# Forming the low half of every fourth transposed block on TensorE and copying it out with ScalarE

## The reference, cut to what matters

```
sc = jnp.einsum('bqkgd,bqjkd->bqkgj', qg, kg).astype(jnp.float32) * scale
sc = jnp.where(valid[:, :, None, None, :], sc, -jnp.inf)
p = jax.nn.softmax(sc, axis=-1).astype(v.dtype)
o = jnp.einsum('bqkgj,bqjkd->bqkgd', p, vg)
```

## Time and profile before

| | us |
|---|---|
| Median of 3 runs | 3589.48 (3582.31, 3589.48, 3591.34) |
| The profiled execution's own time | 3584.13 |
| Its span in the trace | 3582.3 |
| PE busy in the span | 3170.6 (89%) |
| Weight loads busy | 2670.9 (75%) |
| DVE busy | 2083.1 (58%) |
| ACT busy | 1833.1 (51%) |
| POOL busy | 781.8 (22%) |

### The profile page before, as it was taken

One profiled execution on the slowest core, in us unless ns is written; L12 is line 12 of the kernel. 1 busy time (PEld: TensorE's weight loads), 2 busy tenths in 40 slices (PEclk: granted clock), 3 DMA queues, 4 the chain that ended last, 5 costly groups with the idle time before them and its releaser, 6 DMA issues. The chain is left out here.

```text
span 3582.3 us, 51698 instructions
## 1 busy us (share of the span) xinstructions
PE 3170.6 (89%) x17464; PEld 2670.9 (75%) x17464; DVE 2083.1 (58%) x5173; ACT 1833.1 (51%) x3664; POOL 781.8 (22%) x1091
## 2 busy tenths in 40 slices
PE   2999949999949899999399997899969999969998
PEld 1788848888837777778267775899858888859997
DVE  2577648888825556564499986544336666642112
ACT  2566536767735565666377775211136666643221
POOL 1544421111123221211011101111014444311110
PEclk8999979999979999999699998899979999979999
DMA  6466672243172222222621112544342222144332
GB/s 138 144 207 202 194 184 55 57 105 74 38 241 80 77 74 63 78 66 76 120 49 39 29 31 73 168 142 141 124 162 67 70 70 71 41 127 150 118 118 71
DMA packets 345285, 370.25 MB, mean 103 GB/s; under 512 B 68384, under 2 KB 289360, under 8 KB 340288
## 3 DMA queue, kind: packets, MB, share of 16 engines
q1 hardware_dynamic: 331184, 318.39, 32.0%
q0 software_dynamic: 13840, 48.58, 4.2%
HBM read 216.10 MB, written 150.80 MB: 102 GB/s over the span
## 5 line engine op out<-in xcount | busy, mean ns | idle before, releaser
L76 PE MATMUL i_p_g<-i_hT_lo,i_wh 128*128 128x512 f32 x768 | 310.7, 405 | 5.5 <-issue 5.0
L78 PE MATMUL i_p_g<-i_hT_hi,i_wh 128*128 128x512 f32 x768 | 306.9, 400 | 0.0
L77 PE MATMUL i_p_g<-i_hT_hi,i_wl 128*128 128x512 f32 x768 | 306.2, 399 | 0.0
L1509 DVE SCALAR_TENSOR_TENSOR i_score<-i_relu,i_w,i_score 128x1024 f32<-128x1024 f32 (+7 forms) x154 | 156.1, 1024 | 194.5 <-ACT i_relu L1383 192.2
L1394 ACT ACTIVATE i_above<-i_score,i_less 128x384 bf16<-128x384 f32 (+13 forms) x140 | 182.9, 1306 | 91.6 <-POOL i_less L1460 70.9
L1028 DVE TENSOR_TENSOR mla_tl<-mla_p_t,mla_th 128x512 fp32r<-128x512 f32 (+1 forms) x320 | 186.1, 606 | 45.1 <-ACT mla_th L1071 43.2
L998 DVE CUSTOM_DVE_ANT_0 dsa_probs<-dsa_p_s,dsa_mask 128x512 f32<-128x512 f32 (+3 forms) x320 | 184.6, 605 | 42.2 <-PE dsa_p_s L1638 40.6
L1071 ACT ACTIVATE mla_th<-mla_p_t 128x512 fp32r<-128x512 f32 (+1 forms) x320 | 164.2, 530 | 87.2 <-PE mla_p_t L968 84.5
L1383 ACT ACTIVATE i_relu<-i_p_s 128x1024 f32<-128x1024 f32 (+7 forms) x176 | 141.9, 810 | 126.3 <-DVE i_score L1506 84.1
L1028 DVE TENSOR_TENSOR dsa_tl<-dsa_p_t,dsa_th 128x512 fp32r<-128x512 f32 x272 | 179.8, 686 | 37.8 <-ACT dsa_th L1071 32.6
L1637 PE MATMUL dsa_p_s<-dsa_k_hi,dsa_q 128*128 128x512 f32 (+3 forms) x320 | 132.2, 415 | 70.5 <-DMA dsa_k_lo<-scratch_kbT 45.5
(11 more groups left out here) (338 smaller groups left out, 9750.5 us busy)
## 6 DMA issues: line engine op xcount, KB each, us to landing
scratch_gates<-i_ob SPq DMA_DIRECT2D x96, 256.0 KB, 2.4
m_m<-scratch_gates SPq DMA_DIRECT2D x64, 256.0 KB, 4.4
f_hs<-scratch_h2T SPq DMA_DIRECT2D x16, 1024.0 KB, 9.7
scratch_qkT<-b_th SPq DMA_DIRECT2D x64, 192.0 KB, 2.6
scratch_qkT<-b_tl SPq DMA_DIRECT2D x64, 192.0 KB, 3.0
i_ws<-in_w_in SPq DMA_DIRECT2D x24, 512.0 KB, 4.5
b_xt<-in_x SPq DMA_DIRECT2D x16, 512.0 KB, 5.0
scratch_h<-b_xh POOLq DMA_DIRECT2D x16, 512.0 KB, 3.0
```

Of the source, the lines that this page charges most:

```text
L76: pe.matmul(out, l[0], r[1], start=start, stop=False)
L77: pe.matmul(out, l[1], r[0], start=False, stop=False)
L78: return pe.matmul(out, l[0], r[0], start=False, stop=stop)
L1509: nc.vector.scalar_tensor_tensor(out=acc, in0=r, scalar=w[:, t, h:h + 1], in1=acc, op0=ALU.mult, op1=ALU.add).then_inc(summed, 1)
```

## The change

Blocks with b % 4 == 1 are treated otherwise in the sparse stage (`subtract_every = 4`; 68 of the 272). The dense stage has `subtract_every = 0` and keeps its steps.

For such a block the four transposes leave the accumulation in the bank open. Once ACT has made `th`, PE multiplies `th` by a 128 x 128 matrix of minus identity and adds the product into the same bank, one matmul of 512 columns; the bank then holds the low half. ACT copies it to `tl`. DVE does nothing for the block. PE's matmul stands behind the transposes of block b+1 and ahead of the multiplication that follows them; ACT's copy stands behind its copy of block b+1's high half. The matrix is made once at the stage's start, by one ACT instruction of 128 x 128. Whoever waited for the low half of such a block (the multiplication, and `wait_bank`) now waits for ACT's second copy.

```diff
@@ stage_attention
+        minus = sb("minus", [P, P], F32R)
+        on_pe = lambda b: bool(layer.subtract_every) and b % layer.subtract_every == 1
+        def wait_remainder(eng, b):
+            if on_pe(b):
+                eng.wait_ge(copied, n_on_pe(b) + 1)
+            else:
+                eng.wait_ge(lo_done, b - n_on_pe(b) + 1)
@@ tensor
+            def subtract():
+                n, place, j, s0 = to_subtract.pop(0)
+                b = n_b[n] + place
+                pe.wait_ge(minus_made, 1)
+                pe.wait_ge(hi_done, b + 1)
+                nc.tensor.matmul(p_t[:, ring(n, place), s0 * P:GT], minus[:], th[:, b % S, s0 * P:GT], start=False,
+                                 stop=True, skip_group_check=True).then_inc(subtracted, 1)
@@ multiply, wait_bank
-                    pe.wait_ge(lo_done, b + 1)
+                    wait_remainder(pe, b)
@@ step "B"
                     for s in range(s0, 4):
-                        last = nc.tensor.transpose(p_t[:, ring(n, place), s * P:(s + 1) * P],
-                                                   probs[:, n % R, s, j * P:(j + 1) * P], ident[:])
+                        last = nc.tensor.matmul(p_t[:, ring(n, place), s * P:(s + 1) * P],
+                                                probs[:, n % R, s, j * P:(j + 1) * P], ident[:], is_transpose=True,
+                                                start=not stays_open or s == s0,
+                                                stop=not stays_open or s == 3)
                     last.then_inc(turned, 1)
                     behind.append((n, place, j, s0))
+                    if to_subtract:
+                        subtract()
+                    if on_pe(n_b[n] + place):
+                        to_subtract.append((n, place, j, s0))
                     if len(behind) > layer.lag:
                         multiply()
@@ vector, step "B"
+                    if not on_pe(b):
                         (the waits and the subtraction of L1028 as before)
@@ scalar
+            nc.scalar.activation(minus[:], ident[:], ACT.Copy, scale=-1.0).then_inc(minus_made, 1)
+            def copy_remainder():
+                n, place, j, s0 = to_copy.pop(0)
+                b = n_b[n] + place
+                act.wait_ge(subtracted, n_on_pe(b) + 1)
+                nc.scalar.activation(tl[:, b % S, s0 * P:GT], p_t[:, ring(n, place), s0 * P:GT],
+                                     ACT.Copy).then_inc(copied, 1)
@@ scalar, step "B", behind the copy to th
+                    if to_copy:
+                        copy_remainder()
+                    if on_pe(b):
+                        to_copy.append((n, place, j, s0))
@@ class Dsa
+    subtract_every = 4
```

More of the change, by code:

```diff
@@ L791 @@
     depth = 2
+    subtract_every = 0
     def pe_start(self, pe): ...
@@ L890, in stage_attention @@
         stored, lowered = sem(f"{tag}_stored", 2), sem(f"{tag}_lowered")
+        minus_made, subtracted, copied = (sem(f"{tag}_{n}") for n in ("minus_made", "subtracted", "copied"))
+        on_pe = lambda b: bool(layer.subtract_every) and b % layer.subtract_every == 1
+        n_on_pe = lambda b: sum(on_pe(x) for x in range(b))
+        def wait_remainder(eng, b):
[3 more added lines that the diff above has]
+                eng.wait_ge(lo_done, b - n_on_pe(b) + 1)
         n_s = [sum(-(-k // GT) for u in units[:n] for k in u["keys"]) for n in range(len(units) + 1)]
@@ L917, in _ @@
             i = 0
-            behind = []
+            behind, to_subtract = [], []
+            def subtract():
[5 more added lines that the diff above has]
+                                 stop=True, skip_group_check=True).then_inc(subtracted, 1)
             def multiply():
@@ L950, in wait_bank @@
                 else:
-                    pe.wait_ge(lo_done, r - m + 1)
+                    wait_remainder(pe, r - m)
             for step in steps:
@@ L966, in _ @@
                     wait_bank(n, place)
+                    stays_open = on_pe(n_b[n] + place)
                     for s in range(s0, 4):
-                        last = nc.tensor.transpose(p_t[:, ring(n, place), s * P:(s + 1) * P],
-                                                   probs[:, n % R, s, j * P:(j + 1) * P], ident[:])
+                        last = nc.tensor.matmul(p_t[:, ring(n, place), s * P:(s + 1) * P],
+                                                probs[:, n % R, s, j * P:(j + 1) * P], ident[:], is_transpose=True,
+                                                start=not stays_open or s == s0,
+                                                stop=not stays_open or s == 3)
                     last.then_inc(turned, 1)
                     behind.append((n, place, j, s0))
+                    if to_subtract:
+                        subtract()
+                    if on_pe(n_b[n] + place):
+                        to_subtract.append((n, place, j, s0))
                     if len(behind) > layer.lag:
@@ L982, in _ @@
                     last.then_inc(inv_turned, 1)
+            while to_subtract:
+                subtract()
             while behind:
@@ L1024, in _ @@
                     b = n_b[n] + place
[L1025 to L1030, removed]
+                    if not on_pe(b):
+                        if b >= S:
+                            dve.wait_ge(multiplied, b - S + 1)
+                        dve.wait_ge(hi_done, b + 1)
+                        nc.vector.tensor_tensor(tl[:, b % S, s0 * P:GT], p_t[:, ring(n, place), s0 * P:GT],
+                                                th[:, b % S, s0 * P:GT].bitcast(F32),
+                                                ALU.subtract).then_inc(lo_done, 1)
                     if place == 0:
@@ L1079, in _ @@
                                          ACT.Copy).then_inc(spread_done, 1)
+            while to_copy:
+                copy_remainder()
         @block.gpsimd
```

3 lines of the change are left out of this document (2 added, 1 removed).

## The result

The changed kernel takes 3618.57 us (median of 4 runs, 3618.04 to 3624.07); the kernel before takes 3588.39 (median of 4 runs). The ratio is 1.009, with a 95% interval of 1.0072 to 1.0107: 26 to 38 us slower. The profiled executions stand at 3618.21 and 3584.13 us, 34.1 apart. The forecast was 3617.5, +28 on either base.

The account below looks back on a forecast made before the run. PE bounds the mixed phases, DVE the lead phases. Issues 15.6, high-half waits 12, bank 10 + 3, less lead phases 5.5, DVE's lag 4 and earlier exponentials 3 make +28 us on 3589.5: 3617.5, range 3590 to 3635.

Parts of the forecast that it names:

- What bounds the stage: Sparse stage: PE issues without a pause in mixed phases (about 14 us of pauses); in lead phases it waits for DVE.
- The issues, +15.6: PE, sparse stage: 68 new matmuls add 0.23 us each, 15.6 us, none hidden in pauses.
- L939's starts aren't 0.23 us from their follower's: Sign of being wrong: the new matmul on PE not followed by its next start after 0.23 us.
- The wait for the high half, +12: PE's new matmul waits for ACT's copy behind exponentials: 16.7 us read, less 4.5 where PE pauses anyway.
- earlier exponentials: A DVE free earlier makes some shifts and exponentials earlier; a quarter of 20 late places gain 0.6 us, -3 us.
- The bank, +13: PE's transposes wait for banks given back later: 10 us at 8 unit ends, 3 us at 5 places with exponentials.
- DVE's lag, -4: Mixed phases: of 14 us of PE pauses, mostly transposes waiting for a lagging DVE, 4 us are given back.
- The lead phases, -5.5: Behind 8 units whose last block is one of the 68, DVE starts chunks a subtraction earlier: at most 5.5 us gained.
- the 0.3 that I had named as a sign of being wrong: Sign of being wrong: lead phases get shorter by more than 0.3 us in units other than the 8.
- DVE as the limit: Rival: DVE's lag drives PE in both sparse-stage phases; -31 us, 3558; chance 0.13.
- The noise case: Rival: issues cost 15.6 us, waits mostly overlap or ACT catches up, DVE gives back some 10; +5 us, 3594; chance 0.22.
- The bank alone: Rival: the 2.8 us bank chain exceeds 2.9, so all 68 blocks stall at b+3; adds 17 us, 3634; chance 0.07.

Follow-up runs that it names:

- the relief alone: Kernel before without DVE's subtraction for the 68 blocks, PE multiplying by their high half twice; stage -7.1 us, ratio 0.9983.
- the matmuls alone: Kernel before with 68 more 512-column matmuls (zero matrix times high half, into the output bank), no new wait; stage +9.6 us, ratio 1.0027.
- lead 4 and 6: Kernel before with 4 or 6 chunks in the sparse stage's lead phases instead of 8; stage +29.7 us (ratio 1.0079) and +5.8 us (single run).
- the ACT copies alone: Kernel before with 68 more ACT copies of 128x512 from the high half into an unused tile; stage +5.9 us, ratio 1.0016.
- the matmul behind the multiplication: Changed kernel with PE's subtraction behind the multiplication that follows the transposes of b+1, not ahead of it; stage +23.3 us against before, ratio 1.0058.
- no last blocks: Changed kernel with the 8 blocks that end a unit left to DVE, 60 instead of 68; stage +28.4 us against before, single run.
- the placed blocks: Changed kernel with 57 blocks chosen away from exponentials and unit ends instead of 68; stage +13.1 us against before, ratio 1.0030.
- lead 10: Kernel before with 10 chunks in the sparse stage's lead phases instead of 8; stage +16.3 us, ratio 1.0045.
- the last placed kernel: Changed kernel with 57 chosen blocks and PE's subtraction behind the multiplication as well; stage +10.7 us against before, ratio 1.0030.

## Why the prediction was right

**What bounds the stage.** That PE is the limit in the mixed phases held: 68 of DVE's subtractions taken away gave 7.1 us. In the lead phases PE does wait for DVE, but with half of their chunks gone the wait is nearly as long (50.5 for 57.9 us), which points to DVE's late beginning more than to its pace. A further weak spot was small: I had said that no issue falls into a pause, and alone 5.4 us of them do.

**The issues, +15.6.** The step held. Around block 158 in the changed kernel, in order of time (start, duration, instruction, idle before):

```profile
2065.69 0.60 PE L991 MATMUL dsa_p_t<-ident,dsa_probs 128*128 128x128 f32 x4
...
2066.16 1.07 ACT L1114 ACTIVATE dsa_th<-dsa_p_t 128x512 fp32r<-128x512 f32 x2
2066.88 0.47 PE L939 MATMUL dsa_p_t<-dsa_th,dsa_minus 128*128 128x512 f32 x1 [0.59 <-ACT dsa_th L1114]
2067.19 0.39 PE L954 MATMUL dsa_p_o<-dsa_th,dsa_v 128*128 128x512 f32 x1
2067.39 0.60 ACT L1095 ACTIVATE dsa_tl<-dsa_p_t 128x512 fp32r<-128x512 f32 x1 [0.17 <-PE dsa_p_t L939]
2067.42 0.40 PE L956 MATMUL dsa_p_o<-dsa_tl,dsa_v 128*128 128x512 f32 x1
```

L939 is followed after 0.31 us, L954 now after 0.23 where its counterpart took 0.32: the new matmul took the longer start upon itself, as costed, and each adds 0.22 us, 15.0 in all. (The prediction's sign of being wrong, "L939's starts aren't 0.23 us from their follower's", came true by this and says nothing: its own costing had put the 0.32 there and the 0.23 behind it.)

**The wait for the high half, +12.** This is the place of the earlier trace rows. The transposes were issued by 2066.04, L939 started at 2066.88: 0.84 us, where the reading had 0.7. Over all 68 the pauses are 19.8 us, 19 of them over 0.3 (I had read 16.7 us and 20). The step is a term that was mis-sized, for two reasons. I had taken off 4.5 us for pauses that stood there anyway (they show up under DVE's lag, below). And I had let PE start at the very end of ACT's copy, where L939 starts 0.14 us behind it: so in all 43 places in which it waited over 0.05 us. Every place that I had worked out comes out longer by about that: 1.49 for 1.37 us at block 9, 0.84 for 0.7 at 157, 1.22 for 1.08 at 249, and 0.12 at 16 places where the copy had ended just before PE got there. The trace of the kernel before, read again with 0.14 us behind each copy, gives 20.1 us. The changed kernel's own copies give 19.4 us by the same reading, so of the 3 us that I took off for earlier exponentials at most 0.7 shows.

The 0.14 us is not what every start behind a copy takes. In the twelve places where the transposes waited over 0.2 us for ACT's second copy, they start 0.05 us behind its end. L939 has two waits in the kernel (for the matrix of minus identity, and for the high half), and ahead of each L939 the trace has a semaphore instruction on PE's queue (PEldq, its sequencer), here from 2066.77 to 2066.82, between the copy's end at 2066.74 and the weight load at 2066.85:

```profile
L938 PEldq EVENT_SEMAPHORE  x68: 51/51/51, 1767.6 to 2245.3; - x68
```

The matrix is made once, so the first of the two waits could be done once ahead of the stage. Whether that brings the 0.14 down to 0.05, some 4 us over 43 places by estimate, wasn't tried.

**The bank, +13.** This is the place of the earlier trace rows:

```profile
1947.59 0.60 PE L991 MATMUL dsa_p_t<-ident,dsa_probs 128*128 128x128 f32 x4
...
1949.13 0.57 ACT L1114 ACTIVATE dsa_th<-dsa_p_t 128x512 fp32r<-128x512 f32 x1
1949.61 0.58 ACT L1095 ACTIVATE dsa_tl<-dsa_p_t 128x512 fp32r<-128x512 f32 x1
1950.24 0.42 PEld L991 LDWEIGHTS dsa_p_t<-ident,dsa_probs 128*128 128x128 f32 x4 [1.33 <-ACT dsa_tl L1095]
```

The second block's transposes wait 1.33 us for the copy of the last block's remainder, 1.3 as read. The eight such places cost 8.9 us (10 in the forecast), other late banks 2.6 (3).

**DVE's lag, -4 (and the 4.5 taken off the waits).** Of the transposes' 15.4 us of pauses after, 11.5 are for ACT's second copy, and 0.5 are distances stretched by the half clock (below). So of the 12.4 before, nearly all for DVE, 3.4 are left: 9.0 given back, where I had 8.5 in the two terms. The run with the relief alone gave 4.5 of these; the rest comes, as I read it from the matmuls alone, of a PE that gets to the bank later.

**The lead phases, -5.5.** They gave 4.9, but the number is right by luck. I had reasoned that in the 8 units that end with one of the 68 blocks DVE starts on the chunks a subtraction earlier, 0.69 us each. The 8 lead phases gave 2.1 us in all: 1.2 behind block 1, 0.5 and 0.4 behind 181 and 209, while the one behind 41 grew by 0.35 and the rest moved by less than 0.1. Another 2.4 us came behind blocks 3, 8 and 11, which aren't among the 8 (0.5, 1.1 and 0.8 us, more than the 0.3 that I had named as a sign of being wrong). And 4.0 of the 4.9 us are pauses ahead of the V step's transposes in the first, short units, which I hadn't looked at; the chunks gave 1.1. First before, then after:

```profile
PE dsa_p_t L980 <- DVE dsa_inv L1036: 6.8, 6, 1.8
...
PEld dsa_p_t L980 <- DVE dsa_tl L1028: 4.2, 3, 2.2
```

```profile
PE dsa_p_t L1009 <- DVE dsa_inv L1068: 3.3, 3, 1.5
```

With the relief alone the 8 gave 2.0 us and the others 0.7; what more came behind the others in the changed kernel was not tested by itself.

**What wasn't in the sum.** In the last unit PE waits 2.67 us for the last exponential, before and after alike. Before, the granted clock stayed at 1.00 (2.4 GHz) to the stage's end; in the changed kernel the granted clock of the stretch behind it is half (1.2 GHz):

```profile
2230.70:2234.10 3.40, 3.40 (x14) 2.91 (x13) 0.80 (x3) 1.61 (x4) 0.00 (x0) 0.50 0.00 0
```

3.4 us at half speed are up to 1.7 us lost; PE's distances there are longer by 1.4. The same pause stands in ten of the kernels (all but those with lead 4 and 6), 2.67 or 2.72 us long. A dip of 3.4 us begins within 1.5 us of its end in seven: the changed kernel, the 68 matmuls alone, the ACT copies alone, the matmul behind the multiplication, no last blocks, the placed blocks, and lead 10. The kernel before, the relief alone and the last placed kernel have none. The kernel before couldn't tell where such a dip falls.

**The total.** In the stage 15.0 + 19.8 + 11.5 - 9.0 - 4.9 + 1.4 = 33.8 of the 34.1. Against the forecast's +28 that is 0.6 less for the issues, 7.8 more of waiting for the high half, 1.5 less for the bank, 5.0 more given back by DVE's lag, 3 of the exponentials' relief hardly come, 0.6 in the lead phases and 1.4 of clock. Two terms were off by more than half and went against each other (4.5 us of that is one amount that I had booked under the waits instead of under the lag), so part of the agreement is luck. The median moved by 30, nearer to the forecast than the stage's length.

**The rivals.** DVE as the limit: fell (relief alone -7.1, not -47). The noise case supposed that the waits overlap and ACT catches up; they did so only in part: the pauses of PE in the mixed phases grew by 22.8 us, where that rival needed them to grow by none. The bank alone, with all 68 chains late: the weight loads of the transposes wait for ACT's second copy in 13 places, not 68. It was near, though: with the matmul 0.55 us later they wait in 24, most of those that came on top having PE stand for only 0.08 us.

## What to carry to other kernels

Before moving work off an engine because it is busy, find the stretches in which that engine is waited for; the engine that takes the work must have its room in the same stretches. A step that is put on an in-order engine is paid three times: its issue (here 0.22 to 0.23 us), the wait for its input right where it stands (0.3 us on average), and what it delays at the end of the chain that returns a buffer. The first is fixed, the other two follow the place: at 57 chosen places the step cost 0.23 us each in all (13.1 us, with small waits and gains that cancel), at every fourth place 0.50 (34.1 us for 68). When such a wait is worked out from a trace, the handover between the engines goes into every place: here 0.14 us in 43 places were 6 of the 19.8 us. And a total that agrees does not show its terms: look for each gain in the stretch that was to give it.

## What the runs showed of the hardware

A PE pause of 2.67 or 2.72 us at the same place of the program had a stretch of 3.4 us at half clock (1.2 GHz) beginning within 1.5 us of its end in seven kernels, and a granted clock of 1.00 (2.4 GHz) to the stage's end in three. The kernel with lead 4 had six such dips in a stage where the kernel before had none after its first 17 us. A matmul with two waits, behind a semaphore instruction of PE's sequencer, started 0.14 us after the end of the ACT copy that it waited for (43 places), transposes with one wait 0.05 us (12 places).
